# GpSimd makes the copies around the transposing DMAs, and weight pieces are spread between silu and rounding

## The reference

```
def swiglu(h, w_gate, w_up, w_down):
    return (jax.nn.silu(h @ w_gate) * (h @ w_up)) @ w_down
```

## Time and profile before

| | |
|---|---|
| median of 3 runs | 1598.02 us (1595.17 to 1604.24) |
| the profiled execution | 1597.33 us |
| its span | 1595.5 us |
| TensorE busy | 1563.8 us (98%) |
| VectorE busy | 1094.9 us (69%) |
| ScalarE busy | 1008.6 us (63%) |
| GpSimd busy | 96.1 us (6%) |
| HBM read | 329.64 MB, 207 GB/s over the span |

### The profile page before, as it was taken

One profiled execution on the slowest core, in us unless ns is written; L12 is line 12 of the kernel. 1 busy time (PEld: TensorE's weight loads), 2 busy tenths in 40 slices (PEclk: granted clock), 3 DMA queues, 4 the chain that ended last, 5 costly groups with the idle time before them and its releaser, 6 DMA issues.

```text
span 1595.5 us, 21865 instructions
## 1 busy us (share of the span) xinstructions
PE 1563.8 (98%) x7808; PEld 1300.0 (81%) x7808; DVE 1094.9 (69%) x1884; ACT 1008.6 (63%) x1952; POOL 96.1 (6%) x155
## 2 busy tenths in 40 slices
PE   8999999999999999999999999999999999999998
PEld 6887888778888778888777888998788889878886
DVE  5586788777776667678877677767655477575554
ACT  6665577765655555468766564776665478685552
POOL 0000021000000000011110000001100010110000
PEclk9999999999999999999999999999999999999999
DMA  9899874279987899874358997642777555158761
GB/s 306 257 336 298 285 173 141 77 242 287 291 305 171 274 250 304 269 215 145 106 176 270 284 294 242 200 169 93 215 209 221 182 193 210 56 186 241 213 209 49
DMA packets 149515, 344.73 MB, mean 216 GB/s; under 512 B 66848, under 2 KB 67616, under 8 KB 148896
## 3 DMA queue, kind: packets, MB, share of 16 engines
q1 hardware_dynamic: 130416, 290.25, 57.6%
q10 hardware_dynamic: 18992, 53.09, 12.0%
HBM read 329.64 MB, written 1.06 MB: 207 GB/s over the span
## 4 chain that ended last, share of the span: by engine, by line
PE 85%; DVE 6%; DMA 4%; ACT 3%; issue 1%; POOL 1%; ACTq 0%; SPq 0%; DVEq 0%; POOLq 0%
PE PS L1041 24%; PE PS L1042 24%; PE PS L1043 24%; DMA QF<-QF 3%; PE PS L1220 2%; DVE Wl L1930 2%; PE PS L1241 2%; PE PS L1283 1%; DVE QTl L1930 1%; PE PS L1381 1%; PE PS L1382 1%; PE PS L1383 1%; DMA raw<-in_ffn 1%; PE PS L1263 1%; PE PS L1059 1%
## 5 line engine op out<-in xcount | busy, mean ns | idle before, releaser
L1930 DVE TENSOR_TENSOR Wl<-raw,Wh 128x1024 fp32r<-128x1024 f32 (+3 forms) x360 | 354.6, 1030 | 34.3 <-ACT Wh L1519 33.4
L1041 PE MATMUL PS<-Wh,Hh 128*128 128x512 f32 (+1 forms) x824 | 321.8, 390 | 2.8 <-DVE Hl L1990 2.8
L1043 PE MATMUL PS<-Wh,Hl 128*128 128x512 f32 (+1 forms) x824 | 318.9, 387 | 0.0
L1042 PE MATMUL PS<-Wl,Hh 128*128 128x512 f32 (+1 forms) x824 | 318.6, 387 | 0.0
L1519 ACT ACTIVATE Wh<-raw 128x1024 fp32r<-128x1024 f32 (+3 forms) x360 | 305.6, 899 | 18.6 <-PE PS L1043 16.8
L1930 DVE TENSOR_TENSOR QTl<-raw,QTh 128x1024 fp32r<-128x1024 f32 (+3 forms) x236 | 231.7, 1021 | 26.4 <-ACT QTh L1519 25.6
L1041 PE MATMUL PS<-QTh,Hh 128*128 128x512 f32 (+2 forms) x536 | 209.2, 390 | 0.0
L1519 ACT ACTIVATE QTh<-raw 128x1024 fp32r<-128x1024 f32 (+3 forms) x236 | 200.0, 891 | 11.8 <-PE PS L1043 10.1
L1043 PE MATMUL PS<-QTh,Hl 128*128 128x512 f32 (+2 forms) x536 | 207.2, 386 | 0.0
L1042 PE MATMUL PS<-QTl,Hh 128*128 128x512 f32 (+2 forms) x536 | 206.9, 386 | 0.0
L1604 ACT ACTIVATE WK<-PS,st 128x256 f32<-128x256 f32 x88 | 41.5, 472 | 236.3 <-PE PS L1043 236.2
(11 more groups left out here) (239 smaller groups left out, 2329.5 us busy)
## 6 DMA issues: line engine op xcount, KB each, us to landing
raw<-in_ffn SPq DMA_DIRECT2D x392, 512.0 KB, 5.5
BT<-in_ada ACTq DMA_DIRECT2D x96, 512.0 KB, 4.9
raw<-in_win SPq DMA_DIRECT2D x64, 512.0 KB, 4.8
raw<-in_wo SPq DMA_DIRECT2D x32, 512.0 KB, 5.4
raw<-in_win SPq DMA_DIRECT2D x8, 420.0 KB, 4.5
raw<-in_lat SPq DMA_DIRECT2D x6, 512.0 KB, 5.9
raw<-in_ffn SPq DMA_DIRECT2D x8, 256.0 KB, 6.0
BT<-in_nab SPq DMA_DIRECT2D x2, 1024.0 KB, 7.9
```

What stands on the lines that cost most here:

```text
L1041: e.matmul(out_, xh, wh, start=start, stop=False)
L1042: e.matmul(out_, xh, wl, start=False, stop=False)
L1043: return e.matmul(out_, xl, wh, start=False, stop=stop)
L1930: ins = e.tensor_tensor(low(p)[:, cc], raw[p % RAW][:, cc], high(p)[:, cc].bitcast(f32), ALU.subtract)
```

## The change

Pack and mend leave ScalarE's program and stand in GpSimd's, as `tensor_copy`. `with_packs` is applied to GpSimd's order of events instead of ScalarE's. A mended tile has a semaphore of its own (f_mend), for which ScalarE's rounding copy waits, and four buffers instead of two. Before writing to a packed buffer again GpSimd waits for the transfer that read it, and VectorE's product waits for the pack that read its FA buffer three products earlier. In `room`, a gu behind (1, 0) and before (9, 0) has 2 instead of 4, and a turn by DMA has 2 instead of 0: of the pieces that go ahead, two stand before silu and product and two before the two roundings.

More of the change, by code:

```diff
@@ L434, in program @@
             semaphore(n) for n in ("f_mm", "f_silu", "f_mul", "f_turn", "f_hi", "f_z"))
-        f_pack, f_cross = semaphore("f_pack"), [semaphore(f"f_cross{i}") for i in range(4)]
+        f_pack, f_mend, f_cross = semaphore("f_pack"), semaphore("f_mend"), [semaphore(f"f_cross{i}") for i in range(4)]
         ada_in = [semaphore(f"ada_in{i}") for i in range(2)]
@@ L585, in weights_to @@
             for s in range(len(STAGES)):
-                at = -1
                 for i, ev in enumerate(order[s]):
                     top = n
[L589 to L592, removed]
+                    if ev[0] == "parts":
                         top = max(n, 2 * min(NP, first[STAGES[s]] + ev[1]) + ev[2])
@@ L597, in weights_to @@
                         laid = s in ENDS and i >= end_at(order[s])
-                        goal = (0, 12, 16, 16, 16, 18)[at] if s == 0 and at < 6 else n if laid else n + 2 * room(ev)
-                        while top < min(2 * NP, goal) and slot_free[top // 2] <= freed_before[s, at] + own:
+                        goal = (0, 12, 16, 16, 16, 18)[i] if s == 0 and i < 6 else n if laid else n + 2 * room(ev)
+                        while top < min(2 * NP, goal) and slot_free[top // 2] <= freed_before[s, i] + own:
                             top += 2
@@ L1612, in gate @@
                                 allow_slow_non_contiguous=True).then_inc(mod_out, 16)
-            def pack(k, g, t):
[L1616 to L1619, removed]
-            def mend(k, g, t):
[L1623 to L1630, removed]
-            def turn(k, g, t):
-                n, z = turn_no[k, g, t], ring_at((k, g, t))
-                e.wait_ge(f_turn, z + 1)
-                e.activation(ATh[:, n % 4, :], PS[:, 6 + z % 2, 0:256], ACT.Copy).then_inc(f_hi, 1)
+            def turn(k, g, t):
+                n = turn_no[k, g, t]
[8 more added lines that the diff above has]
+                e.activation(ATh[:, n % 4, :], src, ACT.Copy).then_inc(f_hi, 1)
             def exponentials(stage, p, z):
@@ L1862, in act_program @@
                                 triangle()
-                    elif what == "pack":
-                        pack(k, x, y)
                     elif what == "turn":
-                        (mend if by_dma(x) else turn)(k, x, y)
+                        turn(k, x, y)
                         if s == y == 0 and x == 1:
@@ L2466, in pool_program @@
                 for what, x, y, z in POOL_WALK[s]:
-                    if what == "norm":
+                    if what == "pack":
+                        pack(k, x, y)
+                    elif what == "turn" and by_dma(x):
+                        mend(k, x, y)
+                    elif what == "norm":
                         if x:
```

## The result

| | before | after |
|---|---|---|
| median (10 runs each) | 1597.37 us (1589.9 to 1604.2) | 1610.11 us (1606.5 to 1614.8) |
| the profiled execution; its span | 1597.33; 1595.5 us | 1610.45; 1608.3 us |

The ratio is 1.0084, 95% interval [1.0064, 1.0104]: the change makes the kernel 13.4 us slower. That lies in the predicted range (1584 to 1613) but is not the forecast, which was 1600 and "no change that shows".

What follows compares the result with a forecast made beforehand. TensorE, busy 1563.8 of 1595.5 us, was taken as the bound. Longer starts 8.1 us plus holds 2.5 less 8.8 saved gave 1.8 us more than 1597.33: 1599.1, stated as 1600 us, range 1584 to 1613.

Steps and rivals of the forecast that it cites:

- what bounds the kernel and where it would show: TensorE, busy 1563.8 of 1595.5 us; changes would show in its pauses at down products and in low clock.
- the two in the middle: TensorE's pauses at 133 and 597 us would go: 2.55 and 2.56 us, each with 1.1 us of low clock.
- signs of being wrong: The prediction fails if start pauses stay under 1 us, or if pauses turn up in the middle of stages.
- the 2.6 us that the prediction had to spare: Middle of a stage: after two pieces move ahead of VectorE's rounding, 2.6 us stay spare, so no new pause.
- the starts without holds: Moved pieces delay VectorE's second rounding by 1.6 us in f1 and f3, 1.0 in f4 and f5, 0.3 in f2.
- The low clock behind the pauses of f1 and f3: Pauses grown to 2.6 us there would bring matmuls at the lower clock, 1.3 us more each.
- GpSimd beside VectorE: GpSimd copies holding VectorE in the five start chains: 0.5 us each, 2.5 us in all, range 0 to 7.
- rival B: GpSimd starves: mends at stage starts wait until VectorE's burst of pieces ends; 1610 us, chance 0.27 together with C.
- The pause at 35 us: Stage f0: TensorE starts 2.4 us earlier, the second tile gives 0.9 us back; 1.5 us gained.
- A: Rival: the start pauses don't grow and about 3 us of the old ones go too; 1586 us, chance 0.31.
- C: Rival: GpSimd copies take near 1.84 us, giving the same picture as rival B; counted in its chance of 0.27.
- 7 us by it for five starts: By the skill's port rule, each copy could hold VectorE for its own length; the starts then cost 7 us, not 2.5.

Runs made afterwards that it cites:

- e1: The kernel before with only the new numbers in room, pack and mend staying on ScalarE: 1604.08 us, 1.0058.
- e4: The changed kernel with both GpSimd copies replaced by memsets of the same buffers, which read nothing (outputs not the reference's): 1595.44 us, 1.0006.
- e6: e4 with each memset made twice, the second waiting for the first: 1595.63 us, 1.0005.
- e8: The changed kernel with the new room numbers only in the first round of each stage and the old ones in the middle: 1615.46 us, 1.0135.
- e5: e3 with both copies on ScalarE, that is, the kernel before with e3's room: 1590.14 us, 0.9972.
- e11: e9's arrangement of pieces with pack and mend left on ScalarE as in the kernel before: 1582.76 us, 0.9930.
- e9: The changed kernel without the two weight pieces ahead of each feed-forward's second tile, turn (0, 1): 1582.52 us, 0.9922.
- e10: e3 run a second time, beside e9: 1586.56 us, 0.9942.
- e12: e9 run again, beside e11: 1584.85 us, 0.9934.
- e7: e3 with the pack back on ScalarE and only the mend on GpSimd: 1592.78 us, 0.9982.
- e3: The changed kernel with the old room numbers in the first round of each stage, the new ones in the middle: 1587.98 us, 0.9958.
- e2: The changed kernel with the old numbers in room, so only pack and mend move to GpSimd: 1595.19 us, 1.0008.

## Why the prediction was right or wrong

**Right: what bounds the kernel and where it would show.** Five pauses at the stages' starts grew, all ended by VectorE's rounding, and the two in the middle went. One of the prediction's own signs of being wrong came in small, though: a pause turned up in the middle of a stage, 1.02 us at 140.06. e1 has 0.89 us at 132.8, so it needs no GpSimd copies; the 2.6 us that the prediction had to spare there did not hold for every tile.

**Right: the starts without holds.** Forecast 2.6, 2.8, 2.6, 1.2 and 1.2 us (before, plus 1.6, 0.3, 1.6, 1.0, 1.0); e4, which takes the holds away and leaves the rest, has 2.56, 2.56, 2.56, 1.43 and 1.43. The prediction's sum without its hold term is 0.7 us faster than before, e4 measures 1.0 us slower with an interval of -2.1 to 3.8. f4 and f5 are 0.2 us over the forecast, f2 0.2 under it. The low clock behind the pauses of f1 and f3 came as forecast.

**Wrong: the size of "GpSimd beside VectorE".** The prediction put 0.5 us on each start, 2.5 in all, and 0 to 7 for the range, on the ground that one of two copies would fall into an idle stretch of VectorE. There are three copies in the chain of a start, not two (mend (0,1), pack (1,1), mend (1,0), because GpSimd's order sets the next group's copies there), and none falls into idle time: after the change VectorE has hardly any at a start. Changed kernel against e4, the pauses of the starts are larger by 1.50, 2.33, 1.50, 1.20 and 1.21 = 7.7 us, where the prediction had 2.5: this is the term that was mis-sized. Some 0.9 of f2's 2.33 is no hold but the copy itself. The transfer is late in both (9.5 and 9.4 us), but the mend takes 1.13 us where the memset takes 0.31, and VectorE idles 1.10 us ahead of rounding (0,0). That the time still lies in the range is luck in part: the range reached up to 1613 for rival B, whose mechanism did not come, and the 7.7 us lie above the 0 to 7 set for this term.

The whole miss is 13.4 - 1.8 = 11.6 us, of which this makes 5.2. By the ratios e4 takes 13.4 - 1.0 = 12.4 us away (good to some 4 us), so nearly the whole loss goes when memsets stand in the copies' place. But what it takes away in f0 is not shown to be holds, as the next paragraph says. Part of the rest is low clock: the mean granted clock is 0.990 in the changed kernel's profiled execution and 0.995 in e4's.

**Wrong in a smaller part: stage f0.** The pause at 35 us was to shrink by 1.5 us net, from 5.18 to 3.7. It is 5.08 and 1.01, 6.1 together. The rounding that ends it is held (0.97 us where 0.42 is usual), but that is 0.55 us. e1, with no GpSimd copies, has 6.1 us as well, and e6, with no holds, 4.32 and 1.38; e4 has 2.61 and 1.75, and e8, with holds, 3.52 and 1.31. The first transfer lands at 31.16 us in e4, 31.38 in e8, 31.84 in the changed kernel and 32.14 in e6, so a part of these differences goes with the landing. The first pause of e1 and e4 (2.74 and 2.61 us) is near the 2.8 worked out; but for the second tile 0.9 us was too little: its pause is 1.0 to 1.8 us in these four and 3.35 in e1. Further on in f0 stand 2.4 us that the prediction didn't have (1.02, 0.67 and 0.73); e4 and e6 don't have them, e1 does (2.3). Together f0 makes 4.8 us of the miss, and what that depends on stays open; 1.6 us are left for the low clock and the spread.

**Rivals.** A (the starts don't grow) is out: they grow in the changed kernel and, without holds, in e4 as well. B named the right engine pair and nearly the right time, 1610, by the wrong mechanism: no mend waits for a burst. None of the 192 copies takes more than 1.88 us, one piece and itself. B would have had the cost in GpSimd's starvation; it is in VectorE's being held, again and again. C is out: undisturbed copies take 0.61 and 0.75 us, near the 0.7 taken.

The rule in the Trainium skill, "SBUF — State Buffer", section "SBUF: two separate sides", that a VectorE instruction with two SBUF inputs and a GpSimd instruction that reads SBUF exclude each other for a whole instruction, agrees with three measurements here: copies wait for one piece at most, memsets lengthen no piece (1.220 us in e4), and the product with a PSUM operand was never held (0.482), though few of them stood beside a copy. The profile's rows show the holds shorter than the copies: 0.41 us by a pack of 0.61, 0.51 by a mend of 0.75. The prediction had worked out 7 us by it for five starts and not taken it; the starts cost 7.7. That the two are so near is luck in part: it counted two copies at 0.7 us, and there were three at 0.4 to 0.5, and 0.9 us more in f2. The 4.99 us of the earlier trace rows stay unexplained.

**Not settled.** The two pauses at the end of f0 (0.67 and 0.73 us) are not the copies' alone: e1, e5 and e11, with the copies on ScalarE, have both (0.46 to 1.17 us), e9, e10 and e12 only the second, e4 and e6 neither. VectorE stood 2.09 us at the modulation data there, for which it hardly waited before; no run varied that. Late landings are rarer where GpSimd mends in the new middle: 5 of 96 transfers over 6 us in the changed kernel and 5 in e7, 5, 6, 5 and 4 in e3, e9, e10 and e12, against 17 before, 19 in e2, 18 in e8, 12 in e1, 11 in e5 and 15 in e11. But e4 and e6, with GpSimd's memsets in the new middle, have 15 and 9. Why was not pursued.

## What to carry to other kernels

When an engine's queue is reordered, ask of each moved piece whether it fills a wait or stands in the one chain that somebody waits for: here two of four pieces did each, and leaving out the wrong pair turned +0.84% into about -0.7%. Work moved to GpSimd cost nothing here where nobody waited for VectorE, and delayed it in a chain of operations with two SBUF inputs that TensorE waited for; count each copy that falls into such a chain (0.4 to 0.5 us for these), not one or two of them, and look for a place behind the last operation of the chain. The groups of the profile show it at once: same instruction count, longer mean.

## What the runs showed of the hardware

- A GpSimd copy of 128 x 512 uint16 lengthens a VectorE instruction with two SBUF operands by up to 0.41 (pack) or 0.51 us (mend) in the timelines above, and by 0.08 to 0.14 us where a pack stood right ahead of a piece; undisturbed it takes 0.61 and 0.75 us. Over the whole changed kernel that is 39.2 us of VectorE's busy time for 192 copies, 0.2 each.
- GpSimd's memset of 128 x 256 float32 takes 0.313 us and lengthens no piece (1.220 us in e4), done twice neither (1.222 in e6).
- Behind a pause of 1.43 us (e4, f4) and 1.66 us (e9, f2) TensorE's granted clock stayed at 1.00. Behind 2.56 us it fell to 0.50 (e4, f1), but behind 2.63 us in f4 of the changed kernel it stayed at 1.00, and behind 2.64 us in f5 it was 0.66 in the mean of the stretch. A pause's length alone does not tell. The windows of e4, f1 and f4:

```profile
344.60:347.60 3.00, 3.00 (x7) 2.42 (x8) 3.00 (x4) 0.00 (x0) 0.00 (x0) 0.50 1.33 255
...
1134.30:1137.40 3.10, 3.10 (x14) 2.56 (x15) 2.80 (x4) 1.63 (x4) 0.00 (x0) 1.00 1.17 214
```
